# RWKV inverse in a hybrid decoder layer: the two products of a level issued alternately, with the transposed inverse on the other half of the partitions

## The chip, the cores and the metric

The kernel runs on one core of a Trainium2 chip. The metric is the device time of one execution in microseconds, the median of several runs; smaller is better. TensorE is called PE below, its weight loads PEld, VectorE DVE, ScalarE ACT and GpSimd POOL, as the profile calls them. SP is the engine that issues most transfers.

## What is computed

One layer of a decoder trunk for 256 tokens of width 1024, in float32: RMSNorm, one input projection, three mixers side by side (causal pooling, RWKV-7 time mixing, sparse attention), sigmoid merge gates, an output projection, then a mixture of 32 experts. The change concerns RWKV alone, 8 heads of width 64, whose reference is a scan over tokens:

```python
def step(state, inp):
    r_t, w_t, k_t, v_t, kk_t, a_t = inp
    sa = jnp.einsum('bhvk,bhk->bhv', state, -kk_t)
    state = (state * w_t[:, :, None, :] + sa[..., None] * (kk_t * a_t)[:, :, None, :]
             + v_t[..., None] * k_t[:, :, None, :])
    return state, jnp.einsum('bhvk,bhk->bhv', state, r_t)
```

The kernel doesn't scan token by token. It takes chunks of 64 tokens (CH). Within a chunk the dependence of a token on the earlier ones is a triangular 64x64 system for each head, and the kernel builds the inverse of its unit triangular matrix by doubling: from the inverse of the diagonal blocks of size n to that of the blocks of size 2n, in the steps n = 1, 2, 4, 8, 16, 32.

## The kernel before

A tile of 128 partitions holds two chunks, chunk c on partitions 64c to 64c+63, and the 8 heads lie behind one another in the free dimension, 64 columns each. The 256 tokens are two such tiles, i = 0 and 1 (NT = 2), worked one after the other. A PE instruction on 64 input rows and 64 output columns uses a quarter of the 128x128 array; which quarter follows from the partitions of its operands (row half) and of its output (column half).

The function `chunkwise` issues one block: 8 heads times 2 chunks, 16 products of 64x64, into one PSUM bank. In the trace every f32 product is two instructions, so a block shows 32.

The inverse is kept twice: xinv, and its transpose zinv. A level n of the doubling (n = 0 to 4) has three products:

- W = (masked level matrix lmask) and xinv, in `early(step)`. ACT copies it to winv. Waits for xinv (`x_ready`) and lmask (`lmask_ready`, made by POOL).
- X = zinv and winv (n below 4 only), in `late(step)`, into bank 6. DVE adds it to xinv.
- Z = winv and zinv, right behind X, into bank 7. DVE adds it to zinv (`z_ready`).

Before the levels, `seed` has the product XZ, from which DVE makes the first xinv; the first zinv DVE makes in `masked`. Behind the levels, `solve` has w0 (a masked matrix amat times the values vrow, in `early`), which ACT copies into rhs, and xu (zinv and rhs, in `late`), 16 products with a moving operand of 128 columns in two banks. Then come `local` (rx at L807, fc at L891, y at L925 and L929) and `scan` (L823 and L902). The products of the chunks with each other are at L951.

These steps are not alone on PE. The list RWKV_STEPS is walked step by step beside the 24 units (g, u) of attention and beside the projections of the merge gates. A unit's turn on PE is, in this order: `early(step)`, the turning of the attention probabilities (L938, needs DVE), half a share of gate products (L609), `late(step)`, with odd u the weighing of the values (L987, needs ACT's copy of the turned probabilities), with even u the scores (L967), the other half of the gate share. Before a unit with u = 0 stands one more step, with the compressed attention (L997 and L1057) in it. All engines run in program order. DVE has in each step first the RWKV part, then the scaling of the next unit's probabilities (L2007, L1776) and the logits of the one behind (L1995). ACT has first the copy of W, then the exponentials of the next unit (L1577), then the copy of the turned probabilities (L1418).

The diff touches `chunkwise`, `early`, `late` (of PE), `late` (of ACT), `masked` (of DVE) and the plan of banks.

Of the kernel before, what the change touches and what calls it, by code (L numbers as in the profile page):

```python
# [23 lines left out]
ALU = mybir.AluOpType  # L24
# [156 lines left out]
def build_layer(nc, x, params, consts, front, experts, g_final, out, bias_rows):  # L181
    ctx = ExitStack()
    with ctx:
# [216 lines left out]
        def hand_early(step):  # L400
# [5 lines left out]
            elif kind == "finish":  # L406
                hand(f"gup{i}", 6 if i else 7)
            elif kind == "products":
                hand(f"A{i}00", 5), hand(f"A{i}01", 6)
            elif kind == "level":  # L410
                hand(f"W{i}{which}", 5)
            elif kind == "solve":
                hand(f"w0{i}", 5)
            elif kind == "local":
                hand(f"rx{i}0", 5), hand(f"rx{i}1", 6)
            elif kind == "scan" and 2 * i + which < NCH - 1:
                hand(f"st{i}{which}", 5)

        def hand_late(step):
# [9 lines left out]
            elif kind == "level":  # L429
                if which < 4:  # L430
                    hand(f"X{i}{which}", 6)
                hand(f"Z{i}{which}", 7)
            elif kind == "solve":
                hand(f"xu{i}0", 6), hand(f"xu{i}1", 7)
# [145 lines left out]
        def _(pe):  # L580
# [196 lines left out]
            def early(step):  # L777
# [12 lines left out]
                elif kind == "level":  # L790
                    n = which
                    pe.wait_ge(q["x_ready"], 5 * i + n + 1)
                    pe.wait_ge(q["lmask_ready"], 6 * i + n + 2)
                    chunkwise(f"W{i}{n}", lmask[(n + 1) % 2], xinv)
                elif kind == "solve":

                    pe.wait_ge(q["z_ready"], 6 * (i + 1))
                    pe.wait_ge(q["tok_ready"], 4 * (i + 1))
                    chunkwise(f"w0{i}", amat[:, :, 2, :], vrow.rearrange("p (h v) -> p h v", h=RH))
                elif kind == "local":  # L800
# [32 lines left out]

            def chunkwise(name, left, right):

                o = begin(name)
                for h in range(RH):
                    for c in range(2):
                        rows = slice(64 * c, 64 * c + 64)
                        last = pe.matmul(o[rows, h * CH:(h + 1) * CH], left[rows, h, :], right[rows, h, :],  # L840
                                         start=True, stop=True)
                end(last, name)

            def late(step):
# [7 lines left out]
                elif kind == "seed":  # L852


                    pe.wait_ge(q["lmask_ready"], 6 * i + 1)
                    chunkwise(f"XZ{i}", lmask[0], like(cn("eye64")[:, None, :], [P, RH, CH]))
                elif kind == "level":
# [3 lines left out]
                    if n < 4:  # L861
                        chunkwise(f"X{i}{n}", zinv, winv)
                    chunkwise(f"Z{i}{n}", winv, zinv)
                elif kind == "solve":

                    pe.wait_ge(q["rhs_ready"], i + 1)
                    for n in range(2):
                        o = begin(f"xu{i}{n}")
                        for h in range(4):
                            for c in range(2):  # L870
                                rows = slice(64 * c, 64 * c + 64)
                                last = pe.matmul(o[rows, h * P:(h + 1) * P], zinv[rows, 4 * n + h, :],  # L872
                                                 rhs[rows, 4 * n + h, :, :], start=True, stop=True)
# [542 lines left out]
        def _(act):  # L1416
# [133 lines left out]
            def late(step):  # L1550
# [3 lines left out]
                if kind == "turn":  # L1554
                    b0 = full(act, f"tok{i}2")
                    give(copy(vrow, b0[:, :]), "tok_ready", f"tok{i}2")
                    b0 = full(act, f"atok{i}")
                    give(copy(rhs[:, :, 0, :], b0[:, :].rearrange("p (h v) -> p h v", h=RH)), "tok_ready", f"atok{i}")
                elif kind == "solve":
# [209 lines left out]
        def _(dve):  # L1769
# [301 lines left out]
            def masked(i, pair):  # L2071
# [12 lines left out]
                if pair == 1:  # L2084
                    dve.wait_ge(q["lmask_ready"], 6 * i + 1)
                    chain(tt(zinv, lmask[0], like(cn("eye64")[:, None, :], [P, RH, CH]), ALU.add), "z_ready", hold=False)
                for p in range(2):
# [386 lines left out]
```

## Time and profile before

| | |
|---|---|
| median of 3 runs | 663.18 us (661.83 to 668.49) |
| profiled execution | 663.38 us, its span 661.6 us |
| PE busy | 613.7 us, 93% of the span |
| DVE, ACT, POOL busy | 216.3, 141.3, 20.1 us |
| moved from HBM | 157.07 MB |

The profile is of one execution. Its times start with the span. A row of the chain of waits is a piece of the path that ended last, followed back from the end: start, length, engine and line, count of instructions. In rows by time a bracket at the end says how long the engine was idle before and what ended that. Ends of matrix instructions are modelled, so the start of the next block says better how long a block took than its own length.

### The profile page before, as it was taken

The numbers are of one execution on the slowest core, as the hardware profiler recorded it, in microseconds if no ns is written. First come the engines' busy times: TensorE is split into PE (matmuls) and PEld (weight loads), VectorE is DVE, ScalarE is ACT, GpSimd is POOL, SyncE is SP. The second block draws the span as 40 slices with busy tenths as digits, with TensorE's granted clock in tenths as the row PEclk, the third lists the DMA queues.
The fourth block names the chain that finished last, engine by engine and source line by source line (L and its number), as shares of the span: only waits on it lengthen the run. The fifth ranks groups of instructions, "written<-read, shape, count | busy, mean of one in ns | idle before, by whom it ended". The sixth has DMA issues, their size and how long they took to land.

```text
span 661.6 us, 11832 instructions
## 1 busy us (share of the span) xinstructions
PE 613.7 (93%) x4992; PEld 450.1 (68%) x4992; DVE 216.3 (33%) x596; ACT 141.3 (21%) x356; POOL 20.1 (3%) x23
## 2 busy tenths in 40 slices
PE   8999999999999999999999999998999888858684
PEld 8988887888877777877778888886344433413241
DVE  3162548424333565345620122226111212012022
ACT  3010243132224263443531000001201111010013
POOL 1000000000200003000000000000000000000000
PEclk9999999989999999999999999999999999969698
DMA  8484335631211111011136996697999999999993
GB/s 326 185 314 181 127 128 190 259 124 65 85 46 65 66 64 65 12 55 66 64 115 276 423 419 229 255 423 274 398 421 419 421 421 420 420 423 421 421 394 129
DMA packets 27288, 158.96 MB, mean 240 GB/s; under 512 B 2896, under 2 KB 7136, under 8 KB 9440
## 3 DMA queue, kind: packets, MB, share of 16 engines
q1 hardware_dynamic: 24224, 137.71, 53.0%
q10 hardware_dynamic: 3008, 20.45, 7.4%
q8 instruction: 42, 0.69, 0.4%
q14 instruction: 14, 0.11, 0.0%
HBM read 157.07 MB, written 1.07 MB: 239 GB/s over the span
## 4 chain that ended last, share of the span: by engine, by line
PE 67%; issue 31%; ACT 1%; POOL 0%; DVE 0%; POOLq 0%; ACTq 0%; DVEq 0%
PE bank L609 45%; PE bank L840 5%; PE bank L938 3%; PE bank L641 2%; PE bank L967 2%; PE bank L987 2%; PE bank L624 1%; PE bank L997 1%; PE bank L951 1%; PE bank L1057 1%; PE bank L872 1%; PE bank L902 1%; PE bank L1007 1%; PE bank L891 1%; PE bank L1135 0%
## 5 line engine op out<-in xcount | busy, mean ns | idle before, releaser
L609 PE MATMUL bank<-hT,ring 128*128 128x256 f32 x864 | 199.9, 383 | 0.2 <-issue 0.2
L609 PEld LDWEIGHTS bank<-hT,ring 128*128 128x128 f32 x864 | 159.3, 190 | 31.4 <-issue 11.8
L609 PE MATMUL bank<-yT,ring 128*128 128x256 f32 x256 | 55.4, 379 | 0.0
L609 PEld LDWEIGHTS bank<-yT,ring 128*128 128x128 f32 x256 | 48.6, 190 | 6.6
L1418 ACT ACTIVATE work<-bank 128x512 f32<-128x512 f32 (+1 forms) x42 | 21.5, 511 | 110.9 <-PE bank L1239 48.9
L1776 DVE TENSOR_TENSOR work<-bank,table 128x512 f32<-128x512 f32 (+1 forms) x22 | 11.6, 544 | 94.1 <-PE bank L1232 85.5
L1285 PE MATMUL bank<-ring,work 128*32 128x512 f32 (+1 forms) x192 | 32.7, 615 | 10.4 <-DMA yT<-experts 7.2
L1232 PEld LDWEIGHTS bank<-work,tok 128*128 128x128 f32 x256 | 30.2, 192 | 10.0 <-issue 10.0
L1223 PE MATMUL bank<-ring,work 128*32 128x512 f32 x240 | 30.4, 612 | 2.6 <-DMA ring<-experts 2.6
L1232 PE MATMUL bank<-work,tok 128*128 128x128 f32 x256 | 31.5, 278 | 0.8 <-DVE work L1780 0.8
L1577 ACT ACTIVATE tok<-tok,small 128x128 f32<-128x128 f32 (+1 forms) x64 | 28.4, 445 | 14.5 <-DVE small L1995 12.6
L1293 PE MATMUL bank<-work 128*128 128x512 f32 (+1 forms) x68 | 29.9, 581 | 0.5 <-DVE work L2342 0.5
L609 PE MATMUL bank<-ring,work 128*128 128x256 f32 (+1 forms) x144 | 29.0, 358 | 0.0
L1783 DVE SCALAR_TENSOR_TENSOR work<-ring,bank 128x512 f32<-128x512 f32 x12 | 8.2, 687 | 58.7 <-PE bank L609 58.7
L609 PEld LDWEIGHTS bank<-ring,work 128*128 128x128 f32 x144 | 24.9, 190 | 2.8
L1293 PEld LDWEIGHTS bank<-work 128*128 128x128 f32 x68 | 12.2, 189 | 18.4 <-issue 17.3
L1783 DVE SCALAR_TENSOR_TENSOR work<-work,bank 128x256 f32<-128x256 f32 x8 | 3.4, 420 | 63.5 <-ACT work L1706 63.5
L1418 ACT ACTIVATE hT<-bank,table 128x128 f32<-128x128 f32 x12 | 3.6, 367 | 92.4 <-PE bank L1127 86.1
L1285 PEld LDWEIGHTS bank<-ring,work 128*32 128x32 f32 x192 | 8.6, 119 | 20.0 <-issue 17.9
L1995 DVE CUSTOM_DVE_ANT_0 tok<-bank,ring 128x128 f32<-128x128 f32 (+1 forms) x64 | 19.6, 352 | 7.5 <-PE bank L967 7.3
L1593 ACT ACTIVATE ring<-bank,small 128x256 f32<-128x256 f32 x24 | 10.1, 471 | 49.9 <-PE bank L609 49.9
L1418 ACT ACTIVATE t<-bank 128x512 f32<-128x512 f32 x16 | 9.6, 597 | 44.6 <-PE bank L840 26.6
(254 smaller groups left out, 748.3 us busy)
## 6 DMA issues: line engine op xcount, KB each, us to landing
ring<-front SPq DMA_DIRECT2D x47, 1024.0 KB, 4.9
ring<-experts SPq DMA_DIRECT2D x40, 1024.0 KB, 24.4
work<-experts SPq DMA_DIRECT2D x9, 1024.0 KB, 27.6
ring<-experts ACTq DMA_DIRECT2D x8, 1024.0 KB, 13.6
table<-experts SPq DMA_DIRECT2D x6, 1024.0 KB, 27.3
yT<-experts SPq DMA_DIRECT2D x6, 1024.0 KB, 26.8
hT<-experts SPq DMA_DIRECT2D x4, 1024.0 KB, 24.0
work<-experts ACTq DMA_DIRECT2D x3, 1024.0 KB, 27.8
```

The lines of the kernel that those rows point to most:

```text
L609: return first(pe.matmul(o, l, r, start=(k == 0), stop=(k == n - 1)))
L641: return first(pe.matmul(o[0:cols, col + i * P:col + (i + 1) * P], w[:, k, lo:lo + cols], hT[:, k, i * P:(i + 1) * P], start=(k == lo == i ...
L840: last = pe.matmul(o[rows, h * CH:(h + 1) * CH], left[rows, h, :], right[rows, h, :], start=True, stop=True)
L938: last = pe.transpose(o[:, b * P:(b + 1) * P], part, ident)
L967: last = pe.matmul(obank[p][:, hp * S:(hp + 1) * S], qT[rows, 2 * g + hp, i * P:(i + 1) * P], keys, start=True, stop=True)
L1223: last = pe.matmul(bank[4][CAP * e:CAP * (e + 1), :], gath[:, k, CAP * e:CAP * (e + 1)], w[:, e, :], start=(k == 0), stop=(k == KD - 1))
L1232: last = pe.matmul(o, tok[:, i, k * P:(k + 1) * P], sel[:, i, :], start=(i == 0), stop=(i == 1))
L1285: last = pe.matmul(o[CAP * e:CAP * (e + 1), 0:w], ghidT[:, f, CAP * e:CAP * (e + 1)], down[e][:, f, lo:lo + w], start=(f == 0), stop=(f == 1))
L1293: return pe.matmul(total[i][lo // 512][:, lo % 512:lo % 512 + w], wselT[:, i, :], ydown[:, lo:lo + w], start=False, stop=(gang == NGANG - ...
L1418: return act.activation(o, i_, ACT.Copy, scale=scale)
L1577: ins = act.activation(pb, pb, ACT.Exp, scale=-1.0, bias=astat[:, 8 * (n % 2) + b:8 * (n % 2) + b + 1], accum_out=astat[:, 16 + 8 * (n % 2 ...
L1995: ins = dve.tensor_tensor_reduce(prob[:, n % 2, bs], b0[:, bs], back, 1.0, FAR, ALU.add, ALU.min, astat[:, 8 * (n % 2) + b:8 * (n % 2) + b ...
```

## The change

`chunkwise` now takes one or two groups, and issues them alternately: for each head first the two products of one group, then the two of the other. Each group says on which half of the partitions its operands lie for chunk c (`swapped`), and whether the output goes to the other half than the operands' (`crossed`).

zinv and winv hold chunk c on the other half of the partitions, 64(1-c). xinv stays where it was. So W reads its own half and writes the other one, X reads the swapped half and writes back crossed, and Z reads and writes on the swapped half. X (crossed, bank 6) and Z (straight, bank 7) are one call. In level 4, which has no X, the last Z is issued together with w0 (crossed, bank 5), which stood in `solve`; the place of w0 in the plan of banks moves with it. rhs lies swapped too; xu reads it there and writes to the half of chunk c. The first zinv is made by two DVE instructions of 64 partitions in place of one, and ACT's copy of atok into rhs by two in place of one.

```diff
@@ the plan of banks
-            elif kind == "solve":
-                hand(f"w0{i}", 5)
...
                 hand(f"Z{i}{which}", 7)
+                if which == 4:
+                    hand(f"w0{i}", 5)
@@ PE, early(step)
-                    chunkwise(f"W{i}{n}", lmask[(n + 1) % 2], xinv)
-                elif kind == "solve":
-
-                    pe.wait_ge(q["z_ready"], 6 * (i + 1))
-                    pe.wait_ge(q["tok_ready"], 4 * (i + 1))
-                    chunkwise(f"w0{i}", amat[:, :, 2, :], vrow.rearrange("p (h v) -> p h v", h=RH))
+                    chunkwise((f"W{i}{n}", lmask[(n + 1) % 2], xinv, 0, 1))
@@ PE, chunkwise
-            def chunkwise(name, left, right):
-
-                o = begin(name)
+            def chunkwise(*groups):
+
+                into = [begin(group[0]) for group in groups]
                 for h in range(RH):
-                    for c in range(2):
-                        rows = slice(64 * c, 64 * c + 64)
-                        last = pe.matmul(o[rows, h * CH:(h + 1) * CH], left[rows, h, :], right[rows, h, :],
-                                         start=True, stop=True)
-                end(last, name)
+                    for o, (name, left, right, swapped, crossed) in zip(into, groups):
+                        for c in range(2):
+                            half = c ^ swapped
+                            rows = slice(64 * half, 64 * half + 64)
+                            to = slice(64 * (half ^ crossed), 64 * (half ^ crossed) + 64)
+                            last = pe.matmul(o[to, h * CH:(h + 1) * CH], left[rows, h, :], right[rows, h, :],
+                                             start=True, stop=True)
+                        if h == RH - 1:
+                            end(last, name)
@@ PE, late(step)
                     if n < 4:
-                        chunkwise(f"X{i}{n}", zinv, winv)
-                    chunkwise(f"Z{i}{n}", winv, zinv)
+                        chunkwise((f"X{i}{n}", zinv, winv, 1, 1), (f"Z{i}{n}", winv, zinv, 1, 0))
+                    else:
+                        pe.wait_ge(q["tok_ready"], 4 * (i + 1))
+                        chunkwise((f"Z{i}{n}", winv, zinv, 1, 0),
+                                  (f"w0{i}", amat[:, :, 2, :], vrow.rearrange("p (h v) -> p h v", h=RH), 0, 1))
                 elif kind == "solve":
 
                     pe.wait_ge(q["rhs_ready"], i + 1)
+                    pe.wait_ge(q["z_ready"], 6 * (i + 1))
...
-                                rows = slice(64 * c, 64 * c + 64)
-                                last = pe.matmul(o[rows, h * P:(h + 1) * P], zinv[rows, 4 * n + h, :],
+                                rows = slice(64 - 64 * c, 128 - 64 * c)
+                                last = pe.matmul(o[64 * c:64 * c + 64, h * P:(h + 1) * P], zinv[rows, 4 * n + h, :],
@@ ACT, late(step)
-                    give(copy(rhs[:, :, 0, :], b0[:, :].rearrange("p (h v) -> p h v", h=RH)), "tok_ready", f"atok{i}")
+                    for c in range(2):
+                        ins = copy(rhs[64 - 64 * c:128 - 64 * c, :, 0, :],
+                                   b0[64 * c:64 * c + 64, :].rearrange("p (h v) -> p h v", h=RH))
+                    give(ins, "tok_ready", f"atok{i}")
@@ DVE, masked
-                    chain(tt(zinv, lmask[0], like(cn("eye64")[:, None, :], [P, RH, CH]), ALU.add), "z_ready", hold=False)
+                    for c in range(2):
+                        rows = slice(64 * c, 64 * c + 64)
+                        ins = tt(zinv[64 - 64 * c:128 - 64 * c, :, :], lmask[0][rows, :, :],
+                                 like(cn("eye64")[rows, None, :], [64, RH, CH]), ALU.add)
+                        chain(ins, "z_ready" if c else None, hold=False)
```

On PE, at levels 3 and 4 and `solve` of the first tile, before. `t,vraw` is X and `vraw,t` is Z where both stand, `t,work` and a single `t,vraw` are W, `work,ring` is w0; L938 turns probabilities, L987 weighs values, L967 makes scores, L609 is a gate share.

```order
L840 MATMUL bank<-t,vraw 64x64 x16
L840 MATMUL bank<-vraw,t 64x64 x16
L987 MATMUL bank<-tok,vraw 64x2x128 x4
L609 MATMUL bank<-hT,ring 128x256 x3
L840 MATMUL bank<-t,vraw 64x64 x16
L938 MATMUL bank<-table,tok 128x128 x4
L609 MATMUL bank<-hT,ring 128x256 x2
L840 MATMUL bank<-vraw,t 64x64 x16
L967 MATMUL bank<-ring 128x256 x4
L609 MATMUL bank<-hT,ring 128x256 x3
L840 MATMUL bank<-work,ring 64x64 x16
L938 MATMUL bank<-table,tok 128x128 x4
```

The same place on PE in the changed kernel, from the last pair of level 3 on (`chunkwise` is L838 now, and 3 is added to the lines behind it):

```order
L838 MATMUL bank<-t,vraw 64x64 x2
L838 MATMUL bank<-vraw,t 64x64 x2
L990 MATMUL bank<-tok,vraw 64x2x128 x4
L609 MATMUL bank<-hT,ring 128x256 x3
L838 MATMUL bank<-t,vraw 64x64 x16
L941 MATMUL bank<-table,tok 128x128 x4
L609 MATMUL bank<-hT,ring 128x256 x2
L838 MATMUL bank<-vraw,t 64x64 x2
L838 MATMUL bank<-work,ring 64x64 x2
L838 MATMUL bank<-vraw,t 64x64 x2
L838 MATMUL bank<-work,ring 64x64 x2
```

X and Z alternate by two, and w0 has moved from behind the gate share up between the products of the last Z.

On PE, behind level 0 of the first tile, with the semaphores that each row waits for, before (L997 turns compressed probabilities):

```order
L840 MATMUL bank<-t,vraw 64x64 [waits bank_free6,z_ready,w_ready]
L840 MATMUL bank<-t,vraw 64x64 x15
L840 MATMUL bank<-vraw,t 64x64 [waits bank_free7]
L840 MATMUL bank<-vraw,t 64x64 x15
L997 MATMUL bank<-table,xcmp 7x128 [waits bank_free2,cprob_ready,v_ready]
L997 MATMUL bank<-table,xcmp 7x128 x3
L840 MATMUL bank<-t,work 64x64 [waits bank_free5,lmask_ready,x_ready]
```

And in the changed kernel, from the last products of the pair on:

```order
L838 MATMUL bank<-t,vraw 64x64 x2
L838 MATMUL bank<-vraw,t 64x64 x2
L1000 MATMUL bank<-table,xcmp 7x128 [waits bank_free2,cprob_ready,v_ready]
L1000 MATMUL bank<-table,xcmp 7x128 x3
L838 MATMUL bank<-t,work 64x64 [waits bank_free5,lmask_ready,x_ready]
```

Before, the 16 products of Z stood between X and the W that waits for `x_ready`; now only L1000 does.

On DVE, at the first zinv of the second tile (`vraw<-work,table`), before:

```order
L1776 TENSOR_TENSOR vraw<-work,table 128x512
L1776 TENSOR_TENSOR ring<-bank,table 128x2x256 x2
L1776 TENSOR_TENSOR t<-bank,table 128x512
L2007 RECIPROCAL small<-small 128x2
L1776 TENSOR_TENSOR small<-small,gate_t 128x2
L1776 TENSOR_TENSOR tok<-tok,small 128x512
```

and in the changed kernel:

```order
L1782 TENSOR_TENSOR vraw<-work,table 64x512 x2
L1782 TENSOR_TENSOR ring<-bank,table 128x2x256 x2
L1782 TENSOR_TENSOR t<-bank,table 128x512
L2013 RECIPROCAL small<-small 128x2
L1782 TENSOR_TENSOR small<-small,gate_t 128x2
L1782 TENSOR_TENSOR tok<-tok,small 128x512
```

One more instruction stands ahead of the same chain, whose last row makes the probabilities that L941 turns.

## Rows read from the trace of the kernel before

**Rows 1.** The page: PE and the transfer rate in 40 slices
```profile
PE 613.7 (93%) x4992; PEld 450.1 (68%) x4992; DVE 216.3 (33%) x596; ACT 141.3 (21%) x356; POOL 20.1 (3%) x23
GB/s 326 185 314 181 127 128 190 259 124 65 85 46 65 66 64 65 12 55 66 64 115 276 423 419 229 255 423 274 398 421 419 421 421 420 420 423 421 421 394 129
```

**Rows 2.** Windows, 160 to 300 us: length, busy by engine, clock, DMA share
```profile
180.00:190.00 10.00, 10.00 (x190) 8.06 (x186) 2.88 (x5) 2.73 (x10) 1.27 (x1) 1.00 0.31 107
...
sum 140.00, PE 139.89 PEld 110.77 DVE 63.38 ACT 52.55 POOL 14.34; mean PE 9.99 PEld 7.91 DVE 4.53 ACT 3.75 POOL 1.02
```

**Rows 3.** Chain of waits, 130 to 230 us: start, length, engine, line, instructions
```profile
154.88 1.03 PE bank L951 x32
...
174.77 2.01 PE bank L840 x64
...
201.42 1.08 PE bank L840 x32
...
205.06 1.08 PE bank L840 x32
...
207.59 1.89 PE bank L872 x32
...
211.99 0.62 PE bank L807 x32
...
214.50 1.74 PE bank L891 x82
...
220.81 0.47 PE bank L823 x16
...
222.72 0.89 PE bank L902 x16
```

**Rows 4.** By time, level 0 of the first tile: X's start to the next W
```profile
174.70 1.15 PE L840 MATMUL bank<-t,vraw 64*64 64x64 f32 x32
...
175.90 0.69 DVE L1776 TENSOR_TENSOR t<-t,bank 128x512 f32<-128x512 f32 x1 [1.23 <-PE bank L840]
...
176.71 0.60 PE L997 MATMUL bank<-table,xcmp 128*7 128x128 f32 x4
...
177.24 0.27 PE L840 MATMUL bank<-t,work 64*64 64x64 f32 x2
```

**Rows 5.** By time, the first zinv of the second tile and the chain behind it
```profile
250.04 0.69 DVE L1776 TENSOR_TENSOR vraw<-work,table 128x512 f32<-128x512 f32 x1
...
253.54 1.23 DVE L1776 TENSOR_TENSOR small<-small,gate_t 128x2 f32<-128x2 f32 x1
254.81 0.69 DVE L1776 TENSOR_TENSOR tok<-tok,small 128x512 f32<-128x512 f32 x1
...
255.94 0.66 PE L938 MATMUL bank<-table,tok 128*128 128x128 f32 x4
```

**Rows 6.** By time, ACT: copies of half width, the copies behind the turns
```profile
154.91 2.40 ACT L1418 ACTIVATE ring<-bank 64x512 f32<-64x512 f32 x4 [5.60 <-PE bank L609]
...
236.31 1.31 ACT L1418 ACTIVATE work<-bank 128x512 f32<-128x512 f32 x2
...
238.23 0.84 ACT L1593 ACTIVATE ring<-bank,small 128x256 f32<-128x256 f32 x2 [0.61 <-PE bank L609]
```

**Rows 7.** By time, the weighing behind level 1 of the second tile
```profile
265.43 0.57 ACT L1418 ACTIVATE tok<-bank 128x512 f32<-128x512 f32 x1
...
266.51 0.44 PE L987 MATMUL bank<-tok,vraw 128*64 128x256 f32 x2
```

**Rows 8.** By time, the turn behind w0 of the second tile
```profile
288.50 0.69 DVE L1776 TENSOR_TENSOR tok<-tok,small 128x512 f32<-128x512 f32 x1
...
290.31 0.33 PE L938 MATMUL bank<-table,tok 128*128 128x128 f32 x1
```

**Rows 9.** SP's waits in the whole span; windows, 400 to 420 us
```profile
SPq L556 <- PE bank L609: 361.9, 38, 25.4
...
400.00:420.00 20.00, 20.00 (x95) 17.60 (x94) 5.29 (x8) 0.00 (x0) 0.00 (x0) 1.00 0.50 177
```

More of the change, by code:

```diff
@@ L855, in late @@
                     pe.wait_ge(q["lmask_ready"], 6 * i + 1)
-                    chunkwise(f"XZ{i}", lmask[0], like(cn("eye64")[:, None, :], [P, RH, CH]))
+                    chunkwise((f"XZ{i}", lmask[0], like(cn("eye64")[:, None, :], [P, RH, CH]), 0, 0))
                 elif kind == "level":
```

## The prediction

> **What bounds the kernel now.** I read the page first. The matrix engine is busy for 93% of the span, far ahead of the others, and the transfer rate is low in the middle of the kernel and at its ceiling only near the end [rows 1]. The changed instructions lie between 160 and 300 us, so the second view was the table of windows over that stage: in its 140 us PE is busy 139.89, at a granted clock of 1.00 (the upper level, 2.4 GHz), while VectorE works 63 and ScalarE 53 us [rows 2]. The chain of waits then shows what PE's time is made of there, block by block, without a gap [rows 3]. So a microsecond less of PE work in a block is a microsecond off the path, as long as no other engine becomes late. Whether it reaches the end depends on the tail: the expert weights come at 420 GB/s from about 470 us on. But the queue that fetches them fetches the front weights first, and its loop over those is held by PE's progress (38 waits for L609, 361.9 us); between 400 and 420 us the transfers use only half of their capacity [rows 1, 9]. Everything that loads is started by PE's progress, so I let the whole tail move with the stage.
>
> **How fast blocks of small products run.** A 64x64 f32 product is two PE instructions in the trace, so a chunkwise block of 16 products is 32. Such a block alone takes 1.08 us, X and Z one behind the other (64) 2.01 us [rows 3]: the second 32 cost 0.93 us, 29 ns each, and about 0.15 us goes to entering the block. The rows of [rows 3] differ in which corners of the array they use, a corner being a half of the input rows with a half of the output columns. One corner at a time (L902, four products on one corner, then four on another): 16 instructions in 0.89 us, 56 ns. Two corners, straight down (L840, and L823 at 16 in 0.47 us): 29 ns. All four in turn (L807): 32 in 0.62 us, so 0.47 us after the entry, 14.7 ns. L951 and L872 say the same for moving operands of 128 columns: 1.03 us with four corners, 1.89 us with two, for 32 instructions each. A corner thus takes a new instruction every 56 to 59 ns, and corners run beside each other. L891 (48 products, 96 instructions by its loops) changes from the straight to the crossed corners after every six products, and takes 1.74 us, 16.6 ns each after the entry: a less even mixture costs a little.
>
> **Part 1: X and Z interleaved, eight times** (levels 0 to 3 of both halves i). The new order goes row half 1, 0, 1, 0 over four different corners, as evenly as L807. By its rate the pair takes 0.15 + 64 x 14.7 ns = 1.09 us in place of 2.01: 0.92 us less, eight times, 7.4 us. By L891's rate it takes 1.21 us and saves 0.80, 6.4 us. I take L807, since its order is the one that the new code has.
>
> **Part 2: the last Z with w0, twice.** Z and w0 were two blocks of 1.08 us in different places (201.42 and 205.06), 2.16 us together with an entry each. Interleaved they cost 1.09: 1.07 less, twice, 2.1 us (by L891's rate 1.9). Gross gain 9.5 us, at the least 8.3.
>
> **Part 3: one block on two crossed corners.** The ten W blocks and the two xu runs (32 instructions for each half i) keep their instructions, but the corners become crossed. No row shows a crossed pair alone. L891 has one in half of its groups and is still near the four-corner rate, so I price the move at zero; the upper end is in the rival below. That the reads of zinv and rhs lie in the other half changes no count.
>
> **Part 4: halves written apart.** VectorE's first zinv becomes two instructions of 64 partitions, ScalarE's copy of atok too. The width, not the number of partitions, sets their time: four copies of 64x512 take 2.40 us on ScalarE, 0.60 each, and two of 128x512 take 1.31 [rows 6]. So each split adds one instruction, of about 0.65 us on ScalarE and, as for 128x512, of 0.69 on VectorE [rows 5]. ScalarE had 0.61 us of idle time before its next work at 238.23 [rows 6]: covered. On VectorE the first half i is covered too, by a stage in which PE projects for microseconds. In the second, 0.69 us is added at 250.04. Its next work is the chain to the probabilities: an instruction of a few elements takes 1.23 us there, beside an operation of GpSimd's, the product that ends the chain begins at 254.81 and ends at 255.50, and PE turns that tile at 255.94 [rows 5]. Slack 0.44 us against 0.69 more: 0.25, and if GpSimd holds it up longer, a little more. I take 0.35 us.
>
> **Part 5: waits that appear.** X and Z now end together, so X is full later, and VectorE adds X and then Z. Before, the X add began 1.20 us after X had started on PE and the next W came 2.54 us after it [rows 4]. Now X is full after 1.09 plus some 0.15, the add takes 0.69 and ends 1.98 us after the start with the semaphore, while PE has the pair and four turns (0.53) behind it at 1.62: PE waits 0.35 us, once; W and all behind it in PE's queue wait. At the other levels a gate share and more stand between (1.5 us and above), so no wait. Next, what PE meets sooner because it is faster itself. Probabilities turned for attention are ready from the weights copy of ScalarE at 266.00 (265.43 + 0.57), and PE uses them at 266.51 [rows 7]; PE comes 0.92 earlier, ScalarE's chain does not: 0.45 us of wait. The turn at 290.31 has its probabilities at 289.19 [rows 8] and comes 1.07 us sooner as w0 is gone: within 0.1 us. The waits of VectorE's Z add shift by 0.15 us in our favour. At the comparable steps of the other levels the same two starts stand further apart than what is taken from them, so I count nothing there. New waits: 0.35 + 0.35 + 0.45 + 0.1 = 1.25 us.
>
> **The sum.** 9.5 - 1.25 = 8.2 us. The profiled execution took 663.38 us (span 661.6), within 0.2 of the median 663.18: 663.4 - 8.2 gives **655.2 us**, 1.2% less. With L807's rate and no new wait it is 653.9; with L891's rate and all waits 8.3 - 1.25 = 7.05, 656.3.
>
> **A rule against it.** The rows of L840 have both row halves write into one bank, on different partitions, and they overlap: 29 ns against 56 [rows 3]. The new blocks do this in two banks at once, where L807, L951 and L891 give each row half a bank of its own. The Trainium skill, page "TensorEngine Tiling (Array Packing)", section "Gotcha 1: PSUM Pressure", says that different row tiles cannot access the same PSUM bank simultaneously. By that the X pair could not overlap, nor the Z pair, and only an X with a Z would. The trace disagrees already for the pairs of before, so I give it little; what it would give is the first rival.
>
> **Rivals.** *Two at a time only* (0.08): the sharing of banks by both row halves holds the rate at 29 ns. An X/Z pair stays at 2.01 us, the last Z and w0 go from 2.16 to 2.01, 0.3 in all, less the 0.35 of VectorE: 663.4 us. For it: no four-corner row of before has both halves in one bank. Against it: the pair rows do.
> *Crossed pairs don't overlap* (0.04), the slower side: an instruction whose output goes to the other half holds up its crossed partner when both write one bank, as W and xu now do. At 56 ns a W takes 0.15 + 1.79, 0.86 more than now, ten times 8.6; xu, at twice 56, goes from 1.89 to 3.73 in each of two halves, 3.7; X/Z, with one crossed product of 1.94, would gain 0.07 each and the two last 0.22 each, 1.0. Net 11.3 slower, 674.7 us. It decides from some 40 ns per crossed instruction on: there a pair takes 1.43 us and the ten blocks still gain 6.1, while W loses 3.5 and xu 1.6, and the waits take the rest. Against it stands L891.
> *The gain turns into waits* (0.08): four corners work, but the chains of ScalarE and VectorE for the attention, which run beside the levels and don't get faster, hold PE in most levels. At 0.4 us in each of ten blocks that is 4 us off the 8.2: 659.2 us. For it: the slacks of [rows 5, 7, 8] are already short. Against it: VectorE and ScalarE are busy for under half of the stage [rows 2].
>
> **How the numbers follow.** The forecast has 0.80. Its own range is 653.9 to 656.3, and with 1.5 us for the scatter of a median it is 652.4 to 657.8. The third rival lies just above, so 652 to 660 holds both, and leaves out 0.12 and the tails. One per cent of this kernel, about what a measurement tells from no change, is 6.6 us: under 656.55 is faster. The forecast clears that by only 1.3 us, so I leave a good eighth of its 0.80 to "same" and give faster 0.70; same has that eighth, the third rival and the first, 0.25; slower has the crossed pairs and a little more, 0.05.
>
> **What would show it.** In the chain of waits an X/Z block of 64 instructions at 1.1 us (2.0: the first rival), W alone still 1.08 (1.9: the second); w0 gone as a block of its own; VectorE's X add beginning about 1.25 us after the pair; a wait of PE for VectorE before the second W, and one for ScalarE at the weighing that stood at 266.51; the stage from the first level to its end about 8 us shorter and everything behind it shifted by the same, with the wait for the expert weights unchanged. I am wrong if these blocks don't shorten, or if the tail stays where it is in time.

## The result, and the profile after

| | before | after |
|---|---|---|
| median | 663.27 us (4 runs, 661.83 to 668.49) | 656.43 us (4 runs, 654.0 to 658.11) |
| ratio, with its 95% interval | | 0.9879 [0.9839, 0.9919] |
| the same kernel again | 663.47 us (11 runs) | 655.38 us (6 runs), ratio 0.9879 [0.9851, 0.9907] |
| profiled execution, its span | 663.38, 661.6 us | 654.0, 652.1 us |

The change makes the kernel 1.2% faster, 8.0 us of 663.4 by the ratio; both intervals leave out 1. The forecast was 655.2.

The chain of waits of the kernel after, from the first products (L954, L951 of before) to the long run of gate and branch projections, answers to [rows 3, 4, 5, 7, 8]; its columns are start, length, engine and line, instructions (a block of 64 is at times listed with fewer, as x62, where the rows by time show all 64):

```profile
152.96 1.03 PE bank L954 x32
...
172.85 1.10 PE bank L838 x62
173.96 0.02 issue
173.98 0.70 DVE t L1782
174.68 0.04 issue
174.72 1.15 PE bank L838 x32
...
177.28 1.09 PE bank L838 x64
...
196.15 1.09 PE bank L838 x64
...
201.10 1.89 PE bank L875 x32
...
248.02 1.73 DVE tok L1782
249.75 0.04 issue
249.80 0.66 PE bank L941 x4
...
254.97 1.10 PE bank L838 x32
...
258.45 0.49 ACT tok L1421
258.94 0.04 issue
258.99 1.08 PE bank L990 x8
...
279.96 0.60 PE bank L941 x4
...
337.22 86.53 PE bank L609 x400
```

X with Z takes 1.09 us (the row at 177.28) in place of 2.01, the last Z with w0 as much (196.15) in place of two blocks of 1.08. W is still 1.08 to 1.10 and xu 1.89, although their corners are crossed now. In three places of the levels the chain leaves PE where it didn't before: for DVE's add of X at 173.98, for DVE's probabilities at 248.02, and for ACT before the weighing at 258.99. PE's waits of the kernel after between 155 and 295 us (in total, times, longest) say how much is idle:

```profile
PE bank L990 <- ACT tok L1421: 0.4, 1, 0.4
PE bank L838 <- DVE t L1782: 0.2, 1, 0.2
PE bank L941 <- DVE tok L1782: 0.2, 1, 0.2
```

**Where the 9.5 us between the two profiles lie.** The end of the stage in the kernel before stands in this row of its chain:

```profile
347.64 86.53 PE bank L609 x400
```

From the first L951 block to it are 192.76 us before (154.88 to 347.64) and 184.26 after (152.96 to 337.22): 8.50 less. This stage is the change's. Behind it both profiles run the same 86.53 us, and to the end of the span it is 313.96 us before and 314.88 after. Ahead of the stage 1.92 us are gone, where nothing that PE does was edited. The windows from 143 to 149 us (length, busy by engine, clock, DMA share, GB/s), first before and then after:

```profile
143.00:149.00 6.00, 6.00 (x36) 5.87 (x36) 2.38 (x8) 2.67 (x6) 0.00 (x0) 0.72 0.00 0
```

```profile
143.00:149.00 6.00, 6.00 (x42) 5.54 (x42) 2.60 (x9) 3.56 (x7) 0.00 (x0) 1.00 0.00 0
```

In the profile of before the granted clock is at its lower level (1.2 GHz) for a part of this window, just behind 32 instructions with moving operands of only 14 and 30 columns; the 16 turns there took 3.37 us, and 1.86 in the profile of after. That is no part of the change: of the 13 profiles of this study 8 show such a dip (0.55 to 0.73), with and without the change. So below I compare the stage, which repeats to 0.01 us in two profiles of the changed kernel and to 0.11 in two of another, and take the whole times only from several runs.

| kernel | stage begins | its length | from its end to the end of the span |
|---|---|---|---|
| before | 154.88 | 192.76 | 313.96 |
| after | 152.96 | 184.26 | 314.88 |
| after, again | 152.99 | 184.27 | 315.34 |
| X, then Z, crossed | 155.01 | 190.81 | 314.28 |
| alternating, straight | 156.47 | 192.97 | 314.16 |
| changing every two heads | 156.48 | 184.60 | 314.92 |
| changing every four heads | 156.89 | 187.47 | 314.24 |
| w0 apart | 154.62 | 186.53 | 313.65 |
| zinv in four | 153.23 | 186.06 | 314.41 |
| scan and fc reordered | 153.30 | 183.04 | 314.06 |
| the same, again | 155.22 | 183.15 | 313.73 |
| copy first | 156.85 | 183.14 | 313.61 |
| both | 153.27 | 181.65 | 314.98 |

The last column scatters over 1.7 us and doesn't follow the second: what the stage gains, the end keeps. It does lean on the dip: 314.07 us on average in the 8 profiles with it, 314.73 in the 5 without. The only profile of the kernel before has the dip, so that the end costs the change nothing is shown to about 1 us, no closer.

### The profile page after: what moved, and what is told of

Its sections match the earlier page's. It is cut to its first block, busy times and chain, and to the rows that moved or that the text cites. A ratio compares the mean times of both kernels' runs of the same rounds, so it can differ in the third digit from the quotient of the medians.

```text
span 652.1 us, 11844 instructions
## 1 busy us (share of the span) xinstructions
PE 604.6 (93%) x4992; PEld 439.1 (67%) x4992; DVE 217.2 (33%) x598; ACT 142.3 (22%) x358; POOL 20.1 (3%) x23
## 3 DMA queue, kind: packets, MB, share of 16 engines
HBM read 157.07 MB, written 1.07 MB: 243 GB/s over the span
## 4 chain that ended last, share of the span: by engine, by line
PE 62%; issue 31%; DMA 2%; ACT 2%; DVE 1%; SPq 0%; POOL 0%; POOLq 0%; ACTq 0%; DVEq 0%
PE bank L609 43%; PE bank L838 3%; PE bank L941 2%; PE bank L641 2%; PE bank L970 2%; PE bank L990 2%; DMA ring<-front 1%; PE bank L624 1%; PE bank L954 1%; PE bank L1060 1%; ACT tok L1583 1%; PE bank L875 1%; PE bank L1000 1%; PE bank L905 1%; PE bank L1010 1%
## 5 line engine op out<-in xcount | busy, mean ns | idle before, releaser
L609 PE MATMUL bank<-hT,ring 128*128 128x256 f32 x864 | 199.9, 383 | 0.4 <-DMA ring<-front 0.3
L609 PEld LDWEIGHTS bank<-hT,ring 128*128 128x128 f32 x864 | 159.2, 190 | 31.7 <-issue 11.8
L609 PE MATMUL bank<-yT,ring 128*128 128x256 f32 x256 | 55.4, 379 | 0.0
L609 PEld LDWEIGHTS bank<-yT,ring 128*128 128x128 f32 x256 | 48.6, 190 | 6.6
L1421 ACT ACTIVATE work<-bank 128x512 f32<-128x512 f32 (+2 forms) x44 | 22.6, 514 | 107.7 <-PE bank L1242 48.9
L1288 PE MATMUL bank<-ring,work 128*32 128x512 f32 (+1 forms) x192 | 35.4, 662 | 10.4 <-DMA yT<-experts 7.2
L609 PE MATMUL bank<-ring,work 128*128 128x256 f32 (+1 forms) x144 | 29.0, 358 | 0.0
L609 PEld LDWEIGHTS bank<-ring,work 128*128 128x128 f32 x144 | 24.9, 190 | 2.8
L1288 PE MATMUL bank<-hT,work 128*32 128x512 f32 x24 | 14.4, 760 | 6.4 <-DMA ring<-experts 6.4
```

The costliest lines, as they stand in the source:

```text
L609: return first(pe.matmul(o, l, r, start=(k == 0), stop=(k == n - 1)))
L1288: last = pe.matmul(o[CAP * e:CAP * (e + 1), 0:w], ghidT[:, f, CAP * e:CAP * (e + 1)], down[e][:, f, lo:lo + w], start=(f == 0), stop=(f == 1))
L1421: return act.activation(o, i_, ACT.Copy, scale=scale)
```

## The experiments

The theory: a corner of the array takes an instruction every 58 ns, the corners work side by side, and the change gains because four of them do. Rivals: the layout or the turn of banks gains; the gain depends on how finely X and Z alternate.

### X and then Z, in the new layout

```diff
-                        chunkwise((f"X{i}{n}", zinv, winv, 1, 1), (f"Z{i}{n}", winv, zinv, 1, 0))
+                        chunkwise((f"X{i}{n}", zinv, winv, 1, 1))
+                        chunkwise((f"Z{i}{n}", winv, zinv, 1, 0))
...
-                        chunkwise((f"Z{i}{n}", winv, zinv, 1, 0),
-                                  (f"w0{i}", amat[:, :, 2, :], vrow.rearrange("p (h v) -> p h v", h=RH), 0, 1))
+                        chunkwise((f"Z{i}{n}", winv, zinv, 1, 0))
+                        chunkwise((f"w0{i}", amat[:, :, 2, :], vrow.rearrange("p (h v) -> p h v", h=RH), 0, 1))
```

> The changed kernel with its layout (zinv on the other half, W and X crossed) but without the alternation: all of X and then all of Z, and the last Z and then w0, as blocks of their own. My theory (the gain is four corners of the array at work at once, and a crossed pair is as fast as a straight one) expects X and Z together at 2.0 us again in the chain of waits in place of 1.09, the last Z and w0 at 2.0 in place of 1.09, W still 1.08: about 9.2 us more than the changed kernel less the waits that go with it (0.8), so some 8.4 us slower than it and within 1 us of the kernel before. The rival that the new layout itself gives part of the gain (crossed products don't hold each other up, or entering a block is cheaper) expects a block of X or Z below 0.95 us and a time clearly between the two kernels.

Measured: 662.86 us (10 runs), ratio to the kernel before 0.9973 [0.9951, 0.9995], stage 190.81. Its chain shows at one X and Z, and at the last Z with w0:

```profile
174.90 1.84 PE bank L838 x62
...
200.87 1.84 PE bank L838 x62
```

The greater part of the gain goes with the alternation, 6.55 of 8.50 us in the stage. But 2.0 us was expected for a pair, and it is 1.84. X is crossed and Z straight, so Z's first instructions find their corners free while X's last ones run. The rows by time at the first pair show it (`t,vraw` is X, `vraw,t` is Z):

```profile
174.83 0.97 PE L838 MATMUL bank<-t,vraw 64*64 64x64 f32 x26
175.59 0.27 PE L838 MATMUL bank<-vraw,t 64*64 64x64 f32 x2
175.64 0.28 PE L838 MATMUL bank<-t,vraw 64*64 64x64 f32 x3
...
175.77 0.98 PE L838 MATMUL bank<-vraw,t 64*64 64x64 f32 x27
```

Z's first two instructions start when 26 of X's 32 have started; the last six of X, three on each of its corners, start beside the first ones of Z, though all of X stands ahead of Z in the program. In the kernel before, where both are straight, no Z starts ahead of an X:

```profile
194.31 1.15 PE L840 MATMUL bank<-t,vraw 64*64 64x64 f32 x32
195.29 1.10 PE L840 MATMUL bank<-vraw,t 64*64 64x64 f32 x32
```

That is 0.17 us for each of eight pairs and 0.32 for the two last (2.16 before), 2.0 us, and the stage is 1.95 shorter than before. My theory missed this: nearly a quarter of the gain comes with the new layout and without alternation, since PE works a little ahead. The rival that the layout gives a part holds so far; the median too is further from the kernel before than the 1 us expected (1.9).

### Alternating, but straight

The kernel before, with X and Z issued two and two.

```diff
                     if n < 4:
-                        chunkwise(f"X{i}{n}", zinv, winv)
-                    chunkwise(f"Z{i}{n}", winv, zinv)
+                        chunkwise((f"X{i}{n}", zinv, winv), (f"Z{i}{n}", winv, zinv))
+                    else:
+                        chunkwise((f"Z{i}{n}", winv, zinv))
```

> The kernel before with the alternation alone: X and Z issued two and two, but both straight down, so on two corners only, with two banks in turn. My theory expects 2.01 us for the 64 instructions, as before, since each corner takes an instruction every 58 ns whoever it belongs to; time as before, at most 0.5 us more for waits (X full later). The rival that the turn of banks is what lets instructions overlap (in the fast rows of before each row half had a bank of its own, in the slow ones both shared one) expects clearly less than 2.01 us, down to 1.1, and some 7 us less in all.

Measured: 665.52 us (1 run, with the dip), stage 192.97, 0.2 longer than before. In its chain:

```profile
176.36 1.92 PE bank L841 x60
178.28 0.02 issue
178.30 0.70 DVE t L1779
...
181.60 2.01 PE bank L841 x64
```

Two banks in turn on two corners give nothing (2.01 us). The rival with the banks falls. The wait for DVE behind the first pair is here too: it comes from the common end of X and Z.

### A change every two and every four heads

```diff
-                for h in range(RH):
+                for h0 in range(0, RH, 2):
                     for o, (name, left, right, swapped, crossed) in zip(into, groups):
-                        for c in range(2):
+                        for h in range(h0, h0 + 2):
+                            for c in range(2):
...
```

The second kernel has 4 in place of 2.

> The changed kernel, but X and Z change every two heads (8 instructions of one, then 8 of the other) in place of every head. If PE looks ahead far enough, as L891 of before suggests (12 instructions of one pair of corners at a time, 16.6 ns each), the block takes 1.10 to 1.2 us. If it issues strictly in order and starts the next only when its corner is free, 8 instructions on two corners hold the other two for 3 x 58 ns, and the block takes about 1.6 us or more.

> The same with a change every four heads (16 instructions of one pair of corners at a time). A look ahead of at least 16 instructions would give 1.3 us at most (the last run of 16 has no partner, 0.23 us more than even mixture). With strict order it is near 1.85 us. Between these, the block's length tells how many instructions PE holds ready; L891's row says at least 6 for each corner, so I expect about 1.4.

Measured: stages of 184.60 and 187.47 us (657.77 and 660.36 us, 1 run each, both with the dip). The rows of a pair in the chain, every two heads:

```profile
180.79 1.14 PE bank L839 x62
```

and every four:

```profile
181.33 1.49 PE bank L839 x58
```

Neither strict order (1.6 and 1.85) nor a look ahead of 16 instructions (1.3). With the run before, the lengths make a rule: the pair costs 2.01 us without a change of corners, 1.84 with one (X and then Z), 1.49 with three. Each change lets 0.17 us run beside, three instructions on each of two corners, as the rows by time above have it. Seven changes would give 0.80, but four corners with 16 instructions each need 1.09; measured 1.14, and 1.09 with a change at every head. The same rule gives the rows of before that I could only call less even: L891 with seven changes, 0.15 + 96 x 29 ns - 7 x 0.17 = 1.74 [rows 3: 1.74]; L902, one change between single corners, 0.15 + 16 x 58 ns - 0.17 = 0.91 [rows 3: 0.89].

### w0 apart

w0 is back in `solve`, crossed, as a block of its own, and the last Z alone (with its place in the plan of banks).

```diff
+                elif kind == "solve":
+                    pe.wait_ge(q["z_ready"], 6 * (i + 1))
+                    pe.wait_ge(q["tok_ready"], 4 * (i + 1))
+                    chunkwise((f"w0{i}", amat[:, :, 2, :], vrow.rearrange("p (h v) -> p h v", h=RH), 0, 1))
...
-                        pe.wait_ge(q["tok_ready"], 4 * (i + 1))
-                        chunkwise((f"Z{i}{n}", winv, zinv, 1, 0),
-                                  (f"w0{i}", amat[:, :, 2, :], vrow.rearrange("p (h v) -> p h v", h=RH), 0, 1))
+                        chunkwise((f"Z{i}{n}", winv, zinv, 1, 0))
```

> The changed kernel with w0 back in solve, as a block of its own; the last Z is a block of its own too. Expected by my sum: last Z 1.08 and w0 1.08 in place of 1.09 together, 2.1 us longer in the stage, less a wait that falls away (at most 0.2). The rival that w0 gave more than its block, since it stood before the turn of a unit's probabilities on PE, would show in a stage longer by 3 us or more; if the turn had waits instead, in less than 1.5.

Measured: 656.54 us (1 run, with the dip), stage 186.53, 2.27 longer than after. The sum had 2.14; the rivals (3 and more, below 1.5) fall. Yet the first of them holds in small. In the first tile the turn behind w0 takes 0.59 us here, and in the changed kernel, where it stands behind a gate share, 0.44, so w0's move gives 0.15 more there:

```profile
202.51 0.59 PE bank L943 x4
```

```profile
199.79 0.44 PE bank L941 x4
```

In the second tile it doesn't (0.59 here, 0.60 in the row at 279.96 of after), where DVE's probabilities were ready (279.84) only just before the turn began (279.89).

### The first zinv in four

```diff
-                    for c in range(2):
-                        rows = slice(64 * c, 64 * c + 64)
-                        ins = tt(zinv[64 - 64 * c:128 - 64 * c, :, :], lmask[0][rows, :, :],
+                    for c in range(4):
+                        rows = slice(32 * c, 32 * c + 32)
+                        to = slice((32 * c + 64) % 128, (32 * c + 64) % 128 + 32)
+                        ins = tt(zinv[to, :, :], lmask[0][rows, :, :],
...
```

> The changed kernel with the first zinv made in four instructions of 32 partitions in place of two of 64, to weigh the cost of the split on VectorE. My part 4 (every instruction costs its width, 0.69 us, whatever its partitions, and the second tile's chain to the turned probabilities has no slack left) expects 1.4 us more of VectorE's work there, a wait of PE before that turn of about 1.5 us in place of the 0.2 to 0.3 that the changed kernel shows, and the stage longer by about 1.4 us. The rival that GpSimd's operations beside it decide the chain (VectorE stands until they end, wherever it begins) expects the wait to grow by less than 0.7 us.

Measured: 655.49 us (1 run), stage 186.06, 1.80 longer than after. PE's waits in its profile (155 to 295 us):

```profile
PE bank L838 <- DVE t L1782: 1.2, 2, 0.9
PE bank L941 <- DVE tok L1782: 0.9, 2, 0.6
PE bank L990 <- ACT tok L1421: 0.4, 1, 0.4
```

Each instruction of 32 partitions takes the 0.68 to 0.69 us that one of 128 took. The extra 1.4 us arrives on PE in full, but at another place than expected: 0.9 us of it before the first W of the second tile, which waits for xinv, and 0.4 more before the turn. The rival with GpSimd falls. The remaining 0.37 us of the stage lie at the turn behind the second tile's last Z and w0, which the changed kernel reaches without a wait:

```profile
281.96 0.66 PE L941 MATMUL bank<-table,tok 128*128 128x128 f32 x4 [0.30 <-DVE tok L1782]
```

DVE itself stands idle for 0.51 us ahead of this chain, behind its add of Z; why, the trace doesn't show.

### The scan and fc loops in another order

The changed kernel, with two more loops turned: in the scan the row halves alternate, in fc the pair of corners changes after every two products in place of six.

```diff
-                    for p in range(2):
-                        rows = slice(64 * p, 64 * p + 64)
-                        yb = bank[plan[f"y{i}{p}"][0]]
-                        for m in range(4):
+                    for m in range(4):
+                        for p in range(2):
+                            rows = slice(64 * p, 64 * p + 64)
+                            yb = bank[plan[f"y{i}{p}"][0]]
...
-                        for flip in range(2):
-                            for product in range(3):
+                        for product in range(3):
+                            for flip in range(2):
```

> The changed kernel, and two loops put in another order with nothing else changed: the scan's four products of one row half and then four of the other become alternate (two corners in place of one at a time, four blocks), and the six products of fc between changes of corners become two (two blocks). If the length of a block is the largest number of instructions on one corner times 58 ns and 0.15 for the entry, the scan block falls from 0.89 to 0.6 us, fc from 1.74 to 1.55: 1.5 us less in all, and against the kernel before 1.3% less. If turns between row halves on the same output half don't overlap, the scan block stays at 0.89.

Measured: 654.05 us (5 runs), ratio 0.9857 [0.9829, 0.9885]; stage 183.04. In its chain:

```profile
208.34 1.56 PE bank L894 x96
...
216.38 0.61 PE bank L905 x16
```

fc takes 1.56 in place of 1.74 and the scan 0.61 in place of 0.89, as expected from the count on the fullest corner (24 x 58 ns + 0.15 = 1.54; 8 x 58 ns + 0.15 = 0.61). Two row halves on one output half, each with its own bank, do overlap. Of 4 x 0.28 + 2 x 0.18 = 1.48 us the stage keeps 1.22: the waits for ACT behind it grow (1.5 us in four waits between 155 and 345 us, against 1.3 in three).

> The kernel with the scan and fc loops in the other order once more, beside the next one, for a narrower interval: 1.4% below the kernel before.

Measured: 653.99 us (6 runs), ratio 0.9835 [0.981, 0.986], stage 183.15.

### The copy of the turned probabilities first

```diff
-                if n + 1 < len(UNITS):
-                    exps(*UNITS[n + 1])
                 b0 = full(act, f"pT{g}{u}")
                 give(copy(probT[:, n % 2, :], b0[:, :]), "probT_ready", f"pT{g}{u}")
+                if n + 1 < len(UNITS):
+                    exps(*UNITS[n + 1])
                 late(step)
```

> The changed kernel with ScalarE's order turned in each unit: the copy of the turned probabilities first, then the exponentials of the next unit. It tests part 5's reading that PE's waits before the weighing are the exponentials standing ahead of that copy. If so the wait of 0.4 us in the stage and the two of 0.46 and 0.45 behind it go, 1.3 us in all. The rival is that the wait only moves: the exponentials start up to 0.7 us later, and PE waits before the turn of the next unit's probabilities instead; then the stage is as long as before, or longer.

Measured: 655.44 us (1 run, with the dip), stage 183.14, 1.12 shorter than after. Its waits (155 to 345 us):

```profile
PE bank L1000 <- ACTq L1433: 0.7, 1, 0.7
PE bank L941 <- DVE tok L1782: 0.4, 2, 0.2
PE bank L838 <- DVE t L1782: 0.2, 1, 0.2
```

and those of the second profile of the changed kernel:

```profile
PE bank L990 <- ACT tok L1421: 1.3, 3, 0.5
PE bank L1000 <- ACTq L1433: 0.7, 1, 0.7
PE bank L838 <- DVE t L1782: 0.2, 1, 0.2
PE bank L941 <- DVE tok L1782: 0.2, 1, 0.2
```

The three waits for ACT are gone; 0.2 us of them came back before a turn. The reading of part 5 holds: the exponentials that stood ahead of the copy were the wait.

### Both

> The scan and fc loops in the other order and ScalarE's copy first, together. If both are what they seem, some 1.3 us below the former alone, 651 to 653 us by the medians; if the wait only moves, no difference from it.

Measured: 653.14 us (6 runs), ratio 0.9828 [0.9798, 0.9859], stage 181.65: 11.1 us shorter than before and 2.6 shorter than the changed kernel. That is the 1.48 us of the blocks and the 1.12 of the copy: the waits for ACT that took a part of the former are gone. In whole times it is below the changed kernel by about 0.5% (ratios 0.9828 and 0.9879), but the intervals overlap, and against the run beside it (0.9835) the medians don't tell them apart; the stage does.

### The changed kernel again

> The changed kernel once more, unedited, for a narrower interval and a second profile. By its two profiles the stage from the first L951 block to the long run of L609 is 8.5 us shorter; I expect 7 to 8.5 us less than the kernel before in the medians and the same 8.5 us in this stage. The further 1.9 us that the first profile of the kernel before spent ahead of the stage (16 turns in 3.4 in place of 1.9 us, at a lower granted clock) should not belong to the change: absent here in both or present by chance. If the change had a cost in the tail, the part from the end of the gate products on would again be 0.9 us longer than before; if not, the difference changes its sign from run to run.

Measured: 655.38 us, ratio 0.9879 [0.9851, 0.9907], stage 184.27. The part behind the stage was long again (315.34, 1.4 us more than before), which by my expectation speaks for a cost in the tail. But it lies anywhere from 313.61 to 314.98 in the other changed kernels, so I put it down to scatter and to the missing dip; that isn't shown.

## Why the prediction was right

**The rate of four corners** carried the sum, and held: 1.09 us for 64 instructions, to the hundredth, as taken from L807. Taking L807 rather than L891 as the model was right because the order of corners is L807's; the experiments with coarser changes show what L891 lacks. One reading beside it was uneven, though no term of the sum rests on it: the 56 ns of L902 still have the entry of 0.15 us in them. Without it they are 46, less than a corner's 58, since three instructions of its second corner run beside the first. The 29 ns of L823 hold as they are: it stands right behind other small blocks and shows no entry (8 instructions on each corner in 0.47 us).

**Parts 1 and 2** gave 7.4 + 2.1 = 9.5 us. From the blocks measured they are 8 x 0.92 + 2 x 1.07 = 9.5. Left out was that the turn behind w0 loses its own 0.15 us with it when it comes to stand behind a gate share (0.44 in place of 0.59): 0.3 for the two tiles, 9.8.

**Part 3**, crossed pairs at no price: W 1.08 and xu 1.89, right. The rival of crossed pairs that hold each other up falls, and so does the one of two at a time. The rule that the prediction cites for the latter from the Trainium skill ("TensorEngine Tiling (Array Packing)", "Gotcha 1: PSUM Pressure"), that different row tiles cannot access the same PSUM bank simultaneously, doesn't describe these blocks: X and Z each come from both row halves into one bank, on different partitions, and four corners ran at once. Both row halves into one bank and on the same partitions was not tried.

**Part 4**: the split on DVE costs 0.64 us of its chain (7.07 us from the second L951 block to the end of the probabilities before, 248.43 to 255.50, and 7.71 after), and PE's turn came 0.25 us late for it where I had 0.35; the plain difference of the slack, 0.25, would have been right. It also brought DVE's add for xinv close to PE's first W, which the prediction did not look at; the doubled split shows the wait there.

**Part 5**: the prediction reckoned from start to start, so here is how much later each of PE's blocks came than its shortened blocks alone would have it, by the starts in the rows:

| place | predicted | measured |
|---|---|---|
| W behind the first pair | 0.35 | 0.32 |
| turn behind the split | 0.35 | 0.25 |
| weighing in the second tile | 0.45 | 0.47 |
| turn behind the last Z and w0, second tile | 0.1 | 0.16 (0.60 long, 0.44 in the first tile) |
| sum | 1.25 | 1.20 |

The profile's list of waits has less in the first three (0.2 + 0.2 + 0.4), since it begins a wait at the modelled end of the block ahead, and a block behind a wait shows 0.07 us longer in the chain (W 1.15 for 1.08, the turn 0.66 for 0.59, the weighing 1.08 for 1.01). One reason given was wrong: X is not full later. DVE's add of X begins 1.13 us after the start of the pair in the chain (172.85 to 173.98), and it began 1.13 after that of X before (174.77 to 175.90), since the alternating pair takes no longer than X alone did. The wait is there because the 0.92 us of Z no longer stand on PE between X and the next W.

So the stage is 9.8 less 1.2, less 0.1 that the changed kernel loses just before the weighing at 234.42 (not followed up): 8.5, as measured. The sum had 9.5 - 1.25 = 8.2; it was short by the turns behind w0.

**The tail** moves with the stage, as the last column of the table says, to about 1 us. That 655.2 lies so close to the second median, 655.38, is partly luck: the medians of the kernel before were 663.27, 663.47, 664.78 and 665.17 us in four sets of runs.

**Same or faster.** The stage's 8.5 us is 1.3%. The prediction called it faster below 656.55 us; the first median lies 0.12 under that and the second 1.2. The interval of the second measurement, 0.9851 to 0.9907, lies on both sides of 0.99, so even the mark of 1% isn't cleared for certain, and by a mark of 2% the change is "same". Most of the 0.70 on "faster" hangs on the choice of 1%.

## What to carry to other kernels

Cut small products into quarters of the array so that consecutive ones go to all four, and change corners after every product or two: here a block lasted as long as the instructions on its fullest corner, and PE worked only some three instructions per corner ahead. Where the layout forces two corners, a swap of halves in one operand can free the other two; here it cost one more instruction on DVE and one on ACT for each tile. And when one engine becomes faster, look in each step at who delivers what it meets next: four such deliveries, not the work itself, took 1.2 of 9.8 us, and one of them was only a matter of order on ACT.

## What was unexpected of the hardware

- PE starts instructions of a free pair of corners before all of those ahead of them in the program have started, but no more than about three for each corner (0.17 us): 2.01, 1.84, 1.49, 1.14, 1.09 us for the same 64 instructions with 0, 1, 3, 7 and 15 changes.
- The granted clock dips at one place of the kernel (143 to 149 us, behind 32 instructions with moving operands of 14 and 30 columns) in 8 of 13 profiles, and not in the other 5; the start of the stage then lies between 154.6 and 156.9 in place of 153.0 to 153.3 us. Two profiles of kernels that differ nowhere ahead of it can differ by 3.9 us.
- In DVE's chain of the second tile the long instruction moved from a product of 2 columns (1.23 us, [rows 5]) to the one of 512 behind it (1.73 us in place of 0.69), with the chain as a whole longer only by the added instruction. Both times a GpSimd operation runs beside it; that this is the cause isn't shown.
